# Final scaling of a normalised output: two of five row tiles done by ScalarE and GpSimd in place of VectorE

## The reference

```
def rmsnorm(x, g):
    xf = x.astype(jnp.float32)
    y = xf * lax.rsqrt(jnp.mean(xf * xf, axis=-1, keepdims=True) + EPS)
    return (y * g.astype(jnp.float32)).astype(x.dtype)
...
  A final RMSNorm is applied at the end.
  y_prompt (BATCH, SEQ, D_MODEL), y_sample (DEC_BATCH, DEC_SEQ, D_MODEL)
```

## Time and profile before

| what | value |
|---|---|
| median of 3 runs | 3159.37 us (3156.62 to 3159.96) |
| profiled execution, its time | 3161.4 us |
| profiled execution, its span | 3159.6 us |
| busy share of the span | PE 97%, DVE 39%, ACT 19%, POOL 8% |
| mean granted TensorE clock | 0.988 |
| last scaling (L2520, tile 4) | starts 3155.23 us, takes 1.29 us |
| last store issued | 3156.55 us |

### The profile page before, as it was taken

How to read it: one execution, slowest core, us unless ns; L and a number is a source line. 1 busy time by engine, 2 the same in 40 slices (tenths; PEclk the granted TensorE clock), 3 DMA queues, 4 the chain that set the end, 5 groups by cost and what they waited for, 6 DMA issues and landing times.

```text
span 3159.6 us, 43528 instructions
## 1 busy us (share of the span) xinstructions
PE 3069.6 (97%) x18861; PEld 1628.5 (52%) x18861; DVE 1240.8 (39%) x2402; ACT 612.1 (19%) x1358; POOL 242.5 (8%) x391
## 2 busy tenths in 40 slices
PE   7999999999998999999999999999999989999998
PEld 4555565656555444444355546665565464444443
DVE  4459553364353121121154694432644331112123
ACT  3141001143423100000032400011534230000001
POOL 1011000011001000000100100001110010000000
PEclk9999999999999999999999999999999989999999
DMA  7346543522333999999961573544224259999997
GB/s 243 108 128 187 153 139 99 160 95 72 130 127 129 351 396 390 397 394 390 386 185 56 180 192 94 150 140 124 78 72 157 97 177 381 394 397 393 391 402 267
DMA packets 153408, 695.17 MB, mean 220 GB/s; under 512 B 12211, under 2 KB 25751, under 8 KB 125313
## 3 DMA queue, kind: packets, MB, share of 16 engines
q1 hardware_dynamic: 125472, 613.97, 54.2%
q0 software_dynamic: 21312, 62.80, 6.8%
q10 hardware_dynamic: 6432, 15.62, 1.3%
HBM read 618.66 MB, written 73.68 MB: 219 GB/s over the span
## 4 chain that ended last, share of the span: by engine, by line
PE 93%; DMA 3%; ACT 2%; DVE 1%; issue 0%; SPq 0%; POOL 0%; ACTq 0%; DVEq 0%; POOLq 0%
PE unit L1479 14%; PE unit L993 14%; PE unit L942 12%; PE work L1482 11%; PE work L1479 7%; PE unit L1005 4%; PE unit L984 4%; PE unit L1024 4%; PE unit L1351 3%; PE unit L932 3%; PE unit L1304 1%; PE work L1172 1%; PE work L956 1%; PE work L1195 1%; PE unit L1363 1%; PE work L1448 1%
## 5 line engine op out<-in xcount | busy, mean ns | idle before, releaser
L993 PE MATMUL unit<-hT,ring 128*128 128x512 f32 x1024 | 452.6, 595 | 0.0
L1479 PE MATMUL unit<-ring,arena 128*64 128x512 f32 x1568 | 353.9, 597 | 1.4 <-ACT hT L1914 1.4
L993 PEld LDWEIGHTS unit<-hT,ring 128*128 128x128 f32 x1024 | 189.7, 190 | 217.4 <-issue 217.4
L2485 DVE SCALAR_TENSOR_TENSOR arena<-work,arena 32x256 f32<-32x256 f32 x128 | 61.6, 482 | 548.9 <-PE work L1482 547.5
L1482 PE MATMUL work<-ring,arena 128*32 128x256 f32 x4608 | 274.7, 382 | 0.0
L1479 PEld LDWEIGHTS unit<-ring,arena 128*64 128x64 f32 x1568 | 109.9, 137 | 220.7 <-issue 218.5
L942 PE MATMUL unit<-hT,ring 128*128 128x512 f32 x512 | 222.2, 593 | 0.0
L1482 PEld LDWEIGHTS work<-ring,arena 128*32 128x32 f32 x4608 | 137.1, 110 | 159.2 <-issue 80.5
L1953 ACT ACTIVATE arena<-work 128x512 f32<-128x512 f32 x32 | 19.1, 597 | 845.0 <-PE work L1496 845.0
L1581 ACT ACTIVATE xT<-unit 128x512 f32<-128x512 f32 x100 | 59.5, 595 | 598.9 <-PE unit L993 392.9
L1479 PE MATMUL work<-ring,arena 128*64 128x512 f32 x736 | 168.3, 600 | 2.1 <-ACT arena L1954 2.1
(11 more groups left out here) (435 smaller groups left out, 3952.4 us busy)
## 6 DMA issues: line engine op xcount, KB each, us to landing
ring<-in_w_e_gate SPq DMA_DIRECT2D x50, 2048.0 KB, 10.3
ring<-in_w_e_up SPq DMA_DIRECT2D x48, 2048.0 KB, 11.3
ring<-in_w_e_down SPq DMA_DIRECT2D x46, 2048.0 KB, 13.0
ring<-in_w_in SPq DMA_DIRECT2D x32, 2048.0 KB, 15.4
ring<-in_w_ada SPq DMA_DIRECT2D x24, 2048.0 KB, 9.2
arena<-in_w_e_down SPq DMA_DIRECT2D x18, 2048.0 KB, 12.0
arena<-in_w_e_up SPq DMA_DIRECT2D x16, 2048.0 KB, 10.5
arena<-in_w_e_gate SPq DMA_DIRECT2D x14, 2048.0 KB, 11.2
```

Source lines behind the costliest of these rows:

```text
L993: last = mm(bank[:, :], w[:, k, m * P:(m + 1) * P], hT[:, k, 0:TS], start=k == 0, stop=k == KD - 1)
L1479: last = mm(big[SLS * c:SLS * c + SLS, :], x, w[:, kk, 512 * c:512 * c + 512], start=k == 0, stop=k == KD - 1)
L2485: STT(y[SLS:SLS + SLOTP, 256 * c:256 * c + 256], W[5][r, 0:256], gpro[r, e:e + 1], gatep[r, :], ALU.mult, ALU.mult)
```

## The change

For tiles 1 and 3 the final scaling is split over two other engines. VectorE only inverts the root. ScalarE multiplies the tile by that column (an activation Copy with a scale column, in place, L1980 of the changed kernel), after root 2 for tile 1 and after root 4 for tile 3. GpSimd then multiplies by `frow` (a TENSOR_TENSOR of 128x1024 in place, L909). SyncE's stores of tiles 1 and 3 wait for GpSimd. Tiles 0, 2 and 4 stay with VectorE.

```diff
+LAST_POOL = (1, 3)
...
             for t in range(NT):
-                sp.wait_ge(sig["y_ready"], t + 1)
+                if t in LAST_POOL:
+                    sp.wait_ge(sig["y_pooled"], LAST_POOL.index(t) + 1)
+                else:
+                    sp.wait_ge(sig["y_ready"], t + 1 - sum(u < t for u in LAST_POOL))
                 sp.dma_start(O["y_sample"][0, tile_t(t), :] if t < NTS else O["y_prompt"][0], ysum[t])\
                     .then_inc(sig["x_moved"], 16)
...
+            pool.wait_ge(sig["vectors_loaded"], 160 * DEPTH + 16)
+            for i, t in enumerate(LAST_POOL):
+                pool.wait_ge(sig["y_scaled"], i + 1)
+                pool.tensor_tensor(ysum[t], ysum[t], frow, ALU.mult).then_inc(sig["y_pooled"], 1)
...
                 a_(orms[:, t:t + 1], orms[:, t:t + 1], ACT.Sqrt, bias=eps, scale=1.0 / D)\
                     .then_inc(sig["tokens_rooted"], 1)
+                if t - 1 in LAST_POOL:
+                    act.wait_ge(sig["y_inverted"], LAST_POOL.index(t - 1) + 1)
+                    a_(ysum[t - 1], ysum[t - 1], ACT.Copy, scale=orms[:, t - 1:t]).then_inc(sig["y_scaled"], 1)
...
             def finish(t):
                 dve.wait_ge(sig["tokens_rooted"], 2 * DEPTH + t + 1)
+                if t in LAST_POOL:
+                    v_.reciprocal(orms[:, t:t + 1], orms[:, t:t + 1]).then_inc(sig["y_inverted"], 1)
+                    return
                 ch.link(v_.reciprocal(orms[:, t:t + 1], orms[:, t:t + 1]))
```

## The result

The changed kernel takes 3167.17 us in the median of 13 runs (3165.32 to 3172.65), the kernel before 3159.37 in 13 runs on the same chips (3153.4 to 3164.84). The ratio is 1.0028, 95% interval [1.0019, 1.0036]: slower by 7.8 us, where +2.8 was forecast. The profiled execution has a span of 3165.0 us.

What follows compares the result with a forecast made beforehand. TensorE holds 93% of the chain, so only the tail, bound by VectorE then ScalarE's latency, could move. Last scale gives back 0.96, multiplication 3 ends 1.47 later, second store adds 1.36: +2.83 us, median 3162.2, range 3158.4 to 3165.3.

Steps and rivals of the forecast that it cites:

- Multiplication 3 has no cover: End of the tail: GpSimd's multiplication of tile 3 runs with no other work beside it, ending at 3157.99; called the deciding term.
- Scale 4 earlier by 0.96: VectorE's last scale in the tail ends 0.96 us earlier, since VectorE loses two scales of 1.28 us each.
- The second multiplication's end behind the old scale 4, 1.47: GpSimd's multiplication of tile 3 ends at 3157.99, against 3156.52 for VectorE's last scale before: 1.47 us later.
- the hold that I assumed for GpSimd coming second: GpSimd's multiplication of tile 3, ready at 3155.27, waits for VectorE's last scale until 3155.56; without it, 0.33 us less.
- The store pair: SyncE's stores of tiles 3 and 4 leave together and share the transfer engines; the second adds 1.36 us.
- the whole without the drain: The forecast's total change at the kernel's end, which had no term for GpSimd's drain: +2.83 us.
- The Copy of 1.15 us: ScalarE's scaling of a 128x1024 tile, reckoned from Square's 1.05 us plus 0.10 for a scale column: 1.15 us.
- that rival: VectorE's add 4 also waits for GpSimd's first multiplication: +5.35 us, 3164.7; chance 0.10.
- The slow rivals: Two cases slower by over 0.2%: last two stores obstruct each other, or GpSimd must fetch code; together chance 0.07.
- The two stores: Rival: the last two stores obstruct each other, landing after 7.2 us and not 2.6; +6.5 us, 3165.9; chance 0.04.
- stop to fetch code: Rival: GpSimd halts before its first multiplication; 1.9 us hidden, slower than the bound from 5.4; estimate 3166.4; chance 0.03.
- bound of 0.2%: For the whole kernel's time: a measurement can hardly tell less than about 0.2% (6.3 us) from no change.

Runs made afterwards that it cites:

- The early drain: Changed kernel plus a GpSimd drain right behind its five last loads, ahead of its multiplications; ratio to the kernel before 1.0012, tail 19.27 us.
- The late wait alone: Kernel before, with GpSimd only waiting for all five scales behind its loads and executing nothing more; ratio 1.0025, tail 23.41 us.
- the run with tile 1 alone: Changed kernel with a GpSimd drain behind its loads and only tile 1 on ScalarE and GpSimd, tile 3 on VectorE; ratio 1.0001, tail 17.74 us.

## Why the prediction was wrong

**What bounds the kernel.** The choice of the tail was right, and the chain of waits was read rightly as far as it goes. The chain ends with the last instruction that does work; I took the last landing for the end of the span and did not look at what else the end waits for.

**The step that failed** is the sentence "Multiplication 3 has no cover: nothing else is left to do." Something was left: GpSimd's drain. It was in the trace of the kernel before, 13.1 us long, under the line at which the programs end, and hidden by 19 us of other engines' work. The change put a wait in front of it. The replay named what stands behind each wait on VectorE, ScalarE and SyncE, but not the last entry of GpSimd's queue, so the sum has nothing for it. In its place the runs showed a drain that lasts 9.3 us beyond the last multiplication and ends the span. The early drain shows what that cost: 5.2 of the 7.7 us. The late wait alone shows that it suffices: +6.65 us with all else as before.

**The rest of the sum** held. Scale 4 earlier by 0.96: 0.95. The second multiplication's end behind the old scale 4, 1.47: 14.93 us after square 0 against 13.68, so 1.25; it is 0.22 too much, though the hold that I assumed for GpSimd coming second is borne out. The multiplication started 0.40 us before scale 4 ended and took 2.60 us against 2.33 alone, so it lost 0.27 of the 0.40; it ended 2.20 us after scale 4, where I had put 2.43. The store pair, reckoned at 1.36: 1.0 us more to land, and store 4 issued 0.40 us behind the multiplication in place of 0.03, so 1.37. Of the whole without the drain, 2.83: 2.5. The Copy of 1.15 us: 1.13. Add 4 was not held beside GpSimd (1.28 us at 3148.93), so that rival is out; by the Trainium skill, "SBUF — State Buffer", section "Who interferes with whom", a VectorE instruction with at most one SBUF input does not contend with GpSimd (outside its modes that use two ports), and one with two SBUF inputs contends with a GpSimd instruction that reads SBUF. The trace agrees on both (1.28 us for the add, 1.99 for scale 3 in the run with tile 1 alone).

**The slow rivals.** Neither was it. The two stores cost 1.0 us of landing time (3.6 against 2.6), not 4.6. GpSimd made no stop to fetch code: its first multiplication started 0.15 us behind the end of ScalarE's copy. (The prediction's estimate for such a stop adds up to 3166.3 us by its own terms, not 3166.4.) My chance of 0.07 for slower was carried by two mechanisms that did not occur.

**The statistics.** Before's 13 runs reach from 3153.4 to 3164.8, while three had shown 3156.6 to 3160.0. With 13 runs a side, 0.28% is clear of no change (interval from 0.19%), and the 0.12% of the run with the early drain just so (from 0.03%). The prediction's bound of 0.2% for what can be told was too wide.

## What to carry to other kernels

Before work is given to an engine that was idle at the end, look at how its program ends. The drains of all engines stand on one line of the profile, and one that is long but hidden moves to behind the new work. Where GpSimd has issued many transfers, a drain placed in an idle stretch of its own takes the debt off the end (5.2 us here). It needs room: placed behind transfers still on their way it took 11.7 to 14.9 us in these runs. Here it took away a loss and made nothing faster by itself, since the kernel before had its drain hidden. Where tiles are stored by one queue in order, a tile that is finished on a slower path has to come later in that order, or it holds up the ones behind it.

## What the runs showed of the hardware

- With no instruction of its own left to wait for, GpSimd's drain took 0.54 us after 6 transfers issued by it since the drain before, 1.85 after 22, 9.25 after 134, and 9.26 after 300 and after 305, with every one of them long landed. With a clear of 0.10 us before it, it took 9.39. Behind a multiplication it lasted 9.3 us more in the changed kernel, and 0.1 us more where a drain had come before.
- A GpSimd drain that began while its transfers were on their way took longer: 12.2 to 13.1 us behind the five loads, 14.7 and 14.9 between the experts, 11.7 at the start of layer 2.
- GpSimd and VectorE, both with two SBUF inputs, held each other up in both orders, and much alike: the second lost the overlap less 0.1 to 0.2 us. VectorE's scale lost 0.71 us of an overlap of 0.90; GpSimd's multiplication lost 0.21 of 0.32 and 0.27 of 0.40.
- A store of 512 KB took 2.6 us to land by itself, 3.6 us when it left right behind another, and 4.1 as the last of four that left within 2.5 us.
